# Queries of two retrieval heads made token block by token block, and half of the embedding gate moved among the second block's expert rows, which are written out instead of looped

## The reference

```python
q = (h @ w_q).reshape(B, S, 8, 2, 128)              # 8 heads, two halves of a query
s1, s2 = q[..., 0, :] . sub_k1, q[..., 1, :] . sub_k2   # 128 scores each
# top 16 of s1, top 16 of s2, top 16 of their 256 sums: 16 experts per head and token
act = gelu(einsum('thkd,td->thk', u_tab[idx], x))
out = einsum('thk,thkd->td', act * softmax(top_s), v_tab[idx])
h = LayerNorm(alpha*h + out + sigmoid(h @ W_g) * (p @ W_p))
```

## Time and profile before

| what | value |
| --- | --- |
| median of three executions | 1877.73 us |
| the profiled execution's own time | 1876.44 us |
| its span | 1874.6 us |
| PE, DVE, ACT, POOL busy | 91%, 73%, 48%, 37% |
| moved by DMA | 660.59 MB, mean 352 GB/s |
| layer 0: dense part, rows of block 0, rows of block 1 | about 0 to 297, 297 to 625, 625 to 940 us |
| layer 1: the same | about 940 to 1220, 1220 to 1549, 1549 to 1864 us |

### The profile page before, as it was taken

One profiled execution on the slowest core, in us unless ns is written; L12 is line 12 of the kernel. 1 busy time (PEld: TensorE's weight loads), 2 busy tenths in 40 slices (PEclk: granted clock), 3 DMA queues, 4 the chain that ended last, 5 costly groups with the idle time before them and its releaser, 6 DMA issues.

```text
span 1874.6 us, 26250 instructions
## 1 busy us (share of the span) xinstructions
PE 1697.6 (91%) x7264; PEld 981.8 (52%) x7264; DVE 1368.4 (73%) x3501; ACT 901.9 (48%) x2245; POOL 698.3 (37%) x593
## 2 busy tenths in 40 slices
PE   8999999999998778878899999999999988887876
PEld 7987887555443222223389778865544422222222
DVE  5887768877677777776569876688777777777755
ACT  5656544454444444444455665335444454444443
POOL 0110003544444555555411100045444444555554
PEclk9999999999999999999999999999999999999999
DMA  6544769999999999999955447799999999999997
GB/s 248 182 127 138 259 230 415 425 427 426 407 427 427 426 427 428 428 427 425 407 193 174 125 163 243 261 425 427 426 425 416 427 427 422 427 428 427 427 427 300
DMA packets 107304, 660.59 MB, mean 352 GB/s; under 512 B 11952, under 2 KB 12352, under 8 KB 41152
## 3 DMA queue, kind: packets, MB, share of 16 engines
q0 software_dynamic: 75952, 546.57, 69.4%
q1 hardware_dynamic: 31248, 112.74, 17.8%
HBM read 658.20 MB, written 1.06 MB: 352 GB/s over the span
## 4 chain that ended last, share of the span: by engine, by line
PE 59%; DMA 18%; issue 9%; ACT 6%; DVE 6%; POOL 1%; DVEq 1%; ACTq 0%; POOLq 0%; SPq 0%
PE acc L919 17%; DMA cst<-experts_dram,stage 8%; PE psum L751 7%; PE psum L753 6%; PE psum L752 6%; PE psum L782 5%; DMA arena<-experts_dram,stage 5%; PE acc L938 5%; DMA arena<-experts_dram,idxu 4%; PE psum L814 2%; PE acc L751 1%; PE psum L841 1%; PE acc L753 1%; PE acc L752 1%; ACT L1340 1%
## 5 line engine op out<-in xcount | busy, mean ns | idle before, releaser
L938 PE MATMUL acc<-arena 128*128 128x512 f32 x896 | 441.4, 621 | 117.3 <-ACT arena L1346 117.2
L919 PE MATMUL acc<-arena 128*128 128x512 f32 x896 | 406.2, 598 | 25.3 <-ACT arena L1320 25.1
L1751 DVE CUSTOM_DVE_ANT_0 arena<-arena,h 128x1024 f32<-128x1024 f32 x224 | 274.7, 1226 | 139.6 <-DMA arena<-experts_dram,stage 60.3
L938 PEld LDWEIGHTS acc<-arena 128*128 128x128 f32 x896 | 157.8, 193 | 398.8 <-issue 398.6
L676 POOL DMA_INDIRECT arena<-experts_dram,idxu x224 | 255.5, 1141 | 286.4 <-PE acc L919 260.0
L1721 DVE CUSTOM_DVE_ANT_0 arena<-arena,h 128x1024 f32<-128x1024 f32 x224 | 274.5, 1225 | 111.3 <-DMA arena<-experts_dram,idxu 103.6
L699 POOL DMA_INDIRECT arena<-experts_dram,stage x196 | 264.7, 1350 | 201.9 <-PE acc L938 158.7
L919 PEld LDWEIGHTS acc<-arena 128*128 128x128 f32 x896 | 165.0, 190 | 240.1 <-issue 164.0
L1600 DVE TENSOR_TENSOR raw_r<-raw,w_hi_r 128x1024 fp32r<-128x1024 f32 x150 | 177.6, 1220 | 65.2 <-ACT w_hi_r L1226 64.5
L1340 ACT ACTIVATE gel<-dots 128x1 f32<-128x1 f32 x256 | 51.9, 203 | 288.5 <-DVE dots L1751 286.9
L1226 ACT ACTIVATE w_hi_r<-raw 128x1024 fp32r<-128x1024 f32 x152 | 154.1, 1053 | 52.6 <-DMA raw<-weights_dram 52.3
(11 more groups left out here) (304 smaller groups left out, 2751.0 us busy)
## 6 DMA issues: line engine op xcount, KB each, us to landing
raw<-weights_dram SPq DMA_DIRECT2D x168, 512.0 KB, 3.7
arena<-weights_dram SPq DMA_DIRECT2D x20, 512.0 KB, 4.8
w_hi<-weights_dram SPq DMA_DIRECT2D x12, 512.0 KB, 5.6
lnr<-lnrows_dram POOLq DMA_DIRECT2D x4, 1024.0 KB, 6.9
arena<-experts_dram,idxu POOLq DMA_INDIRECT x224, 11.9
arena<-experts_dram,stage POOLq DMA_INDIRECT x222, 13.9
lnr<-cum_dram POOLq DMA_DIRECT2D x2, 1024.0 KB, 8.7
cst<-weights_dram SPq DMA_DIRECT2D x4, 512.0 KB, 5.5
```

The source lines that it names most:

```text
L919: last = mm(acc[:, c * 512:(c + 1) * 512], diag[:, i % 4, :], slots[n % RING][:, D + c * 512:D + (c + 1) * 512], start=n == 0, stop=n == R ...
L938: last = mm(acc[:, c * 512:(c + 1) * 512], diag[:, i % 4, :], slots[i % RING][:, D + c * 512:D + (c + 1) * 512], start=False, stop=ends)
L1751: nc.vector.tensor_tensor_reduce(slots[i % RING][:, 0:D], slots[i % RING][:, 0:D], h[:, b, :], 1.0, 0.0, ALU.mult, ALU.add, dots[:, i:i + ...
```

## The change

Four things, in the retrieval of both layers:

- Heads 3 and 5 (`APART`) get their queries one token block at a time, with matmuls of 128x128 instead of 128x256: block 0's among block 0's rows, block 1's queries and scores among block 1's rows (after rows 2, 5, 8 and 20, 23, 26).
- The embedding gate is made one token block at a time. Block 1's second half of the channels goes to rows 40 to 58 of block 1; `base` of block 1 is added to `acc` at row 66 of block 1 (`BASE_AT`) instead of ahead of its row 0.
- The table of what stands beside block 0's rows is laid out anew.
- Block 1's rows are written out on PE, ACT, DVE and POOL, as block 0's are: the copies to `stage`, `wst` and `sl` and the no-operations are gone.

The places of weights follow: head 3's pieces are now loaded late into the spare buffers where head 4's went, and head 4's early where head 3's went; all pieces of the embedding gate are now held until the step that fills `("pg", c, 1)`.

```diff
-    beside = {(0, 1): [("sc", 0, 2), ("sc", 1, 2)], (0, 6): [("wqh", 1, 1)], (0, 9): [("wq", 1, 1)], (0, 11): [("sc", 0, 3), ("sc", 1, 3)]}
-    halves_at, gate_at = (20, 25, 31, 36, 42, 47, 53, 58), (70, 75, 80, 85, 91, 96, 101, 106)
...
-    beside |= {divmod(62 + 3 * b, TOPK): [("pp", 0, b), ("pp", 1, b)] for b in range(2)}
-    beside |= {divmod(n, TOPK): [("pgw", j // 4, j % 4)] for j, n in enumerate(gate_at)}
...
-    s += [("ln2", 0), ("experts", 1), ("ln2", 1)]
+    first[1] = [("sc", b, 2) for b in range(NB)]
+    apart(first, 0, 3, (6, 9, 12))
+    together(4, (16, 21, 24))
+    apart(first, 0, 5, (28, 31, 34))
+    together(6, (38, 43, 46))
+    together(7, (50, 55, 58))
+    for b in range(NB):
+        first[62 + 4 * b] = [("pp", c, b) for c in range(2)]
+    gated_embedding(first, 0, range(NB), (70, 72, 75, 77, 80, 82, 85, 87))
+    gated_embedding(first, 1, (0,), (92, 96, 100, 104))
+    apart(second, 1, 3, (2, 5, 8))
+    apart(second, 1, 5, (20, 23, 26))
+    gated_embedding(second, 1, (1,), (40, 46, 52, 58))
+    for n in range(RANKS):
+        s += [("row", *divmod(n, TOPK))] + first.get(n, [])
+    s += [("ln2", 0), ("experts", 1)]
+    for n in range(RANKS):
+        s += [("row1", *divmod(n, TOPK))] + second.get(n, [])
+    s += [("ln2", 1)]
...
+            def query_side(L, b, hd, ps, i):
+
+                w = whole(L, *QUERY_PIECES[hd][i])
+                for k in range(KT):
+                    last = mm(ps[:, i * P:(i + 1) * P], w[:, k * P:(k + 1) * P], h1w[:, k, b * P:(b + 1) * P], start=k == 0, stop=k == KT - 1)
+                return last
...
+                    if kind == "row1":
+                        _, r, i = step
+                        n = r * TOPK + i
+                        n0 = (L * NB + 1) * RANKS
+                        if n == BASE_AT:
+                            pe.wait_ge(base_ready, L * NB + 2)
+                            for c in range(2):
+                                mm(acc[:, c * 512:(c + 1) * 512], ident, base[:, 1, c * 512:(c + 1) * 512], start=False, stop=False)
...
-                        with pe.Fori(0, EH - 1) as r:
-                            for i in range(TOPK):
-                                weigh(r, i, False)
...
-                        with pool.Fori(0, EH - 1) as r:
-                            for i in range(TOPK):
-                                at_row = number(r, i)
-                                nc.gpsimd.indirect_dma_start(slots[i % RING][:, :], None, experts[:, :], at_row).then_inc(slot_in[i % RING], 16)
...
+                        for n in range(RANKS, NB * RANKS):
+                            if n % HALF == 0:
+                                pool.wait_ge(idx_ready, 2 * L * NB * EH + n // HALF + 1)
...
+                            pool.wait_ge(row_used, L * NB * RANKS + n + 1)
```

More of the change, by code:

```diff
@@ L152, in steps, with apart @@
-    beside |= {divmod(62 + 3 * b, TOPK): [("pp", 0, b), ("pp", 1, b)] for b in range(2)}
-    beside |= {divmod(n, TOPK): [("pgw", j // 4, j % 4)] for j, n in enumerate(gate_at)}
-    beside |= {divmod(gate_at[4 * c + 3] + 1, TOPK): [("pg", c, 0), ("pg", c, 1)] for c in range(2)}
-    for r in range(EH):
-        for i in range(TOPK):
-            s += [("row", r, i)] + beside.get((r, i), [])
-    s += [("ln2", 0), ("experts", 1), ("ln2", 1)]
+    first, second = {}, {}
+    def apart(beside, b, hd, rows):
+        for kind, n in zip(("qbh", "qb", "sc"), rows):
+            beside[n] = [(kind, b, hd)]
@@ new lines, in together, with gated_embedding @@
+    def together(hd, rows):
+        for kind, n in zip(("wqh", "wq"), rows):
+            first[n] = [(kind, hd // 2, hd % 2)]
+        first[rows[2]] = [("sc", b, hd) for b in range(NB)]
+    def gated_embedding(beside, c, blocks, rows):
+        for n, (j, b) in zip(rows, itertools.product(range(4), blocks)):
+            beside[n] = [("pgw", c, j, b)]
+            if j == 3:
+                beside[n + 1] = [("pg", c, b)]
+    first[1] = [("sc", b, 2) for b in range(NB)]
+    apart(first, 0, 3, (6, 9, 12))
@@ L168, in rows_later @@
     out, held = [], []
-    first = STEPS.index(("wqh", 1, 0))
+    first = STEPS.index(("row", 0, 0))
     for step in STEPS[first:]:
@@ L174, in rows_later @@
         out.append(step)
-        if step[0] == "row":
+        if step[0] in ("row", "row1"):
             for wait in held:
@@ L205, with query @@
 NBANK = 6
+def query(b, hd):
+    return ("qb", b, hd) if hd in APART else ("wq", hd // 2, hd % 2) if hd else ("wq0", b)
 def group_list():
@@ L230, in group_list @@
         if hd:
-            made = ("wq", hd // 2, hd % 2)
-            g.append(([made], False, [made, made]))
+            made = [query(b, hd) for b in range(NB if hd in APART else 1)]
+            g.append((made, False, [made[-1], made[-1]]))
         else:
@@ L955, in _ @@
+                    if kind in ("qbh", "qb"):
+                        _, b, hd = step
+                        bk, use = place(L, query(b, hd))
+                        if kind == "qbh":
+                            pe.wait_ge(bank_drained[bk], use)
+                        last = query_side(L, b, hd, psum[:, bk, :], int(kind == "qb"))
+                        if kind == "qb":
+                            last.then_inc(bank_filled[bk], 1)
                         continue
@@ L1174, in _ @@
                         _, b, hd = step
-                        pe.wait_ge(*drained(L, ("wq", hd // 2, hd % 2) if hd else ("wq0", b)))
+                        pe.wait_ge(*drained(L, query(b, hd)))
                         at_hd = 0 if hd == 0 else hd - 1
@@ new lines, in _ @@
+                    if kind == "row1":
+                        _, r, i = step
+                        weight(L, 1, r, i)
+                        if i == 12 and r < EH - AHEAD:
+                            shifted_exp(L, EH + r + AHEAD)
+                        if (r, i) == (EH - 2, 2):
+                            roots()
+                            act.wait_ge(var_ready, L * 4 + 3)
+                            inv_sqrt(rstd[:, :], mv[:, 1:2], mv[:, 1:2], rstd_ready)
+                        if (r, i) == (EH - 1, 5) and L + 1 < DEPTH:
+                            for q in range(2):
+                                columns_hi(L + 1, 0, q)
```

321 lines of the change are left out of this document (122 added, 199 removed).

## The result

The kernel after takes 1889.47 us, the median of four executions (1888.36 to 1890.48), beside 1877.51 us (1876.51 to 1878.03) for the kernel before in the same session: a ratio of 1.0063 (95% interval 1.0051 to 1.0076), 12.0 us slower. The forecast was 1873.9 us and the range ended at 1878.5.

What follows compares the result with a forecast made beforehand. DMA's transfer of expert rows at 427 GB/s was taken to pace both blocks. Against the profiled execution, 1876.4 - 3.5 - 0.4 - 0.6 + 0.7 = 1872.6 us, as a median 1873.9; range 1871.0 to 1878.5.

Steps and rivals of the forecast that it cites:

- G: Block 1's rows written out: about 0.16 MB more fetched code per layer costs 0.7 us in all, bounds 0 and 1.5.
- A: Block 0's new table: lower peak of PE's lag fills the DMA shortfalls at 472 and 1400 us, gaining 3.5 us.
- B: Change of blocks: identity matmuls and index copy gone, PE earlier at rows 0 and 1, a gain of 0.4 us.
- C: Block 1's other additions: 15.8 us more PE work fits into 62 us free there and costs nothing.
- D: Gate in more pieces: four ACT table loads more per layer, 5.1 us, hidden while each pause stays below the 9.5 us queue.
- E: Late and early weight pieces: bytes on SyncE's queue unchanged, last gate piece loaded in time, so nothing either way.
- F: Loops gone: copies and no-operations dropped, gaining only in each layer's last rows, 0.6 us in all, bounds 0 and 1.0.
- R2: Rival, chance 0.06: block 1's fetched code all comes through one DMA engine that paces every row, 12 us slower, 1885 us.

## Why the prediction was wrong

Three steps failed. A line that changes ACT's order ahead of row 0 had no term in the sum and was so put at nothing; it costs 5.9 us. The upper bound of term G, 1.5 us, was too low; the straight code costs 5.4. Term A took a dip in GB/s for lost time; filling it gave nothing of its 3.5 us.

**What the 12.0 us are.** 5.9 us are the ACT copies ahead of row 0 (taking that line back gives 5.9, adding it to the kernel before costs 8.3). 5.4 us are the straight code of block 1, and with the loop kept on VectorE alone hardly any of it is left (ratio 1.0004). The remaining 0.7 us are the sum of the new table, the block-by-block pieces, the gate and the change of blocks, and can't be told from nothing, since each of these numbers is good to some 2 us; with the local pauses mended the new order stands at 1882.4 us, and the old order with the same straight code at 1882.5. So the reordering itself brought nothing that can be measured.

**A, the dips** (3.5 us of gain). Right about the place: at 472 and 1400 us the rate went to 426 or 427. Wrong about the worth. The table and moves as a whole gave no gain, the zero matmuls and the earlier gate each removed dips and no time, and the two spread tables gave +1.5 and -0.4 us. The step that failed is the equation of a dip in GB/s with lost time, "20 x (427 - 381) / 427". A reading that fits is that one share of the rows' transfers is late anyway, and that a short pause is time in which it catches up. That one share is late is seen in the chains of packets above; that it catches up in a pause was not followed. (A slip without weight: 8.67 us for five rows is 1.73 us a row and not 1.72, so PE wins 0.72 us per row.)

**B, the change of blocks** (0.4 of gain). Wrong in sign, by 3.7 us in the rates (2.4 and 1.3), though filling most of it moved no time. I counted 1.7 us of identity matmuls as removed work. They had also split the pause: before, PE waited 1.43 and 1.08 us around them; without them it waited 3.85 us at a stretch, and the next twelve records took 8.41 us, where twelve take 5.32 at 641.7 us at full clock.

**C and D** (nothing). Nearly right in time, not in mechanism. D priced each pause with one sigmoid at 3.2 us and compared it with the queue. Row 60 has a softmax's exponential as well, so three loads stand within 4.7 us, and PE idles 3.52 us and falls to half clock. Moving the gate by four rows took the dips away, and the median fell by 0.4 us, inside the spread. The drain that the Trainium skill counts beside a load (ScalarE: Activation LUTs, "What ACT_TABLE_LOAD costs") isn't seen after either: the load of 1.28 us at 311.09 has the next instruction 0.02 us behind it.

**E, F** (0 and -0.6). E looked at SyncE's queue alone; no part looked at ACT's order ahead of row 0, which the moved anchor of `rows_later` changes. My list of parts was made from the diff's purpose and not from its lines, so 5.9 us had no term at all. F can't be told apart: PE, POOL and ACT written out give ratios of 1.0002, 0.9996 and 0.9996, each with 1 inside its interval.

**G, fetched code** (+0.7, bounds 0 and 1.5). The count of packets was near (17 in block 1 of layer 0, where I had some 21; 0.12 MB more for 0.16), the price was off by seven times: 5.4 us, and 9.4 with VectorE written out by itself. What failed is the upper bound, "the whole difference in pace between 426 in straight code and 427 in loops". A rate in GB/s can't see this cost: 427 holds for 172 us while rows get later by 1.0 us with each VectorE packet. The page of the Trainium skill that I cited (Runtime: NRT & Kernel Launch, "Instruction fetch mechanics"), by which crossing a block of code is mostly hidden, holds here for PE, POOL and ACT, whose written-out code cost nothing measurable; for VectorE's the measurement differs (9.4 us).

**R2** was the rival nearest to the truth: a single late share sets the pace. I gave it 0.06, for block 0 fetches 0.22 MB and runs at 426. That evidence was void twice. The rate doesn't show the cost, and block 0 was paying it already: it has the steps of 1.0 us, and rolling up half of its heads on VectorE gained 3.0 us. The packets bear R2's core out: every row waits for its latest share, and code that comes through that engine sets all later rows back. R2's size (12 us) was wrong, since it put all code on one engine, where VectorE's comes through the late chain and ACT's and PE's through others.

**Open.** Why VectorE's code comes through the chain that is last, and why the row packet behind a code packet takes 0.84 to 0.90 us there and 0.55 to 0.62 in ACT's chain, isn't shown. Nor is how early the other chains are: ACT's five packets held its chain up by 2.9 us in all without a row waiting for it, so more such code might cost too. Also open is why VectorE alone written out costs 9.4 us and all four 5.4. The former keeps its no-operations, so that its code is longer, and its packets come 43 to 45 us apart, where those of all four come 47 to 60; but this was not tried by itself.

## What to carry to other kernels

In a stage paced by many equal transfers, watch the times at which whole transfers complete (the first and the last of a group, and single ones against an even pace), not GB/s: the rate stayed at 427 while rows lost 1.0 us at each fetch of VectorE code. A fetch costs when it falls to the DMA engine whose share of a row is last, and not otherwise. Read every line of a diff that touches the order of an engine's queue, above all an index or an anchor, and ask which instruction now stands ahead of the first one that frees a slot. Before a loop is written out to save hand-overs, it is to be tried on one engine at a time; three of them cost nothing measurable here, the fourth cost 9.4 us, and rolling up its straight code elsewhere gained 3.0 us.

## What the runs showed of the hardware

- A fetch of VectorE's code, one packet of 8 KB on q14 and 0.31 us of one DMA engine, sets a saturated stream of row gathers back by 1.0 us; written-out code on PE (16 KB packets on q8) and on POOL and ACT (8 KB packets on q14, as VectorE's) costs nothing measurable (intervals between 0.9987 and 1.0011).
- Over 180 to 200 us the code packets of VectorE lie in one chain of packets and those of ACT in another, and the row packet behind one is slow: 0.84 to 0.90 us for 0.31 behind VectorE's, 0.55 to 0.62 behind ACT's. Only the chain that finishes each row last costs time.
- In a stage bound by DMA, an idle stretch of PE of 3.06, 3.52, 3.85 or 4.20 us was followed by half clock (two rows in 5.37 instead of 3.69 us), and so were some of 2.02 and 2.09 us, while one of 3.19 us was not. In the kernel before this cost nothing (0.79 of the clock at 429 GB/s). Four zero-by-constant records in the middle of a pause kept the clock at 1.00 and changed the time by nothing.
- Dips in the DMA rate are not additive with the time: at the change of blocks dips of 2.4 and 1.3 us were filled but for 0.4, others grew later in the block, and the gain was nothing.
